# Two DiT blocks on one core: order of the first loads and of VectorE's first work

## The chip, the cores and the metric

The kernel runs on one core of one Trainium2 chip. The metric is the device time of one execution in microseconds (us). The engines of the core are TensorE (PE, matmuls, with its weight loads shown apart as PEld), VectorE (DVE), ScalarE (ACT), GpSimd (POOL) and SyncE (SP), which here only issues transfers (DMAs).

## The reference, cut to what matters

Two transformer blocks run one after the other on x of shape (1, 256, 1024), all in float32. Each has a feed-forward part, a mixing part and a second feed-forward part, and each part starts from a normalised x that is modulated by a scale and a shift computed from the vector c:

```
mods = (jax.nn.silu(c) @ w_ada[l] + b_ada[l]).reshape(B, N_MOD, D_MODEL)
n = modulate(rmsnorm(h, g_pre[l, 0]), shift(0), scale(0))      # x * (1 + scale) + shift
f = swiglu(n, w_ffn_gate[l, 0], w_ffn_up[l, 0], w_ffn_down[l, 0])
h = h + 0.5 * gate(0) * rmsnorm(f, g_post[l, 0])
```

The first matmul of the first feed-forward part therefore needs shift(0) and scale(0), that is silu(c) times the first 2048 columns of w_ada (1024 x 9216). The mixing part of the first block is an attention with a relative bias of 32 buckets, whose table is turned into Toeplitz rows at the start of the program; the rest of the program isn't touched by the change.

## The kernel before, in words

The 256 tokens are two tiles of 128 (T = 2), the model width 1024 is eight blocks of 128 (KD = 8). Weights are cut in pieces of 128 x 2048, loaded into w_raw (three slots) or e_raw, split into a rounded part (w_hi, by ScalarE) and a remainder (w_lo, by VectorE), and multiplied in three products on TensorE.

The program is written by hand, one instruction stream for each engine, with semaphores between them. The opening is the first 50 us or so:

- SP issues loads in the order in which they are written. All of SP's loads go through one queue (q1 in the profile), ScalarE's loads through another (q10).
- The first modulation is made in two halves of 512 columns of shift and of scale. Each half has eight "rows": row j holds w_ada's rows p*8 + j for all 128 partitions p, 128 x 1024 numbers, 512 KB (load_first, line 653). In the first half VectorE sums rows 0 to 6, each multiplied with a column of silu(c) (first_rows, lines 1525 to 1534), and TensorE sums row 7 (first_row, line 2173). In the second half VectorE has rows 0, 1, 4, 5, 6 and TensorE rows 2, 3, 7. The order lists are ON_DVE and ON_PE (lines 319 and 320).
- The sums over partitions are folded: VectorE reduces to 128 x 32 (line 1539, semaphore folded) and TensorE multiplies with the constant matrix pick (line 2171). VectorE then forms mod_col (lines 1549, 1557, 1559, semaphore first_mods), and normalised, transposed tokens go into nT (line 1276 on VectorE, line 881 on ScalarE).
- Tokens: both tiles of x are loaded into x_res (line 671, 512 KB each). ScalarE waits for both, squares them (line 865), GpSimd makes the reciprocal root, ScalarE scales them into y_row (line 1012). TensorE transposes y_row (line 1986).
- The small constants: ScalarE issues c_in, rel_in and onehot, makes silu(c) (c_act, semaphore c_ready), and issues ten more small loads (vec_rows, line 1002). VectorE spreads the relative bias table into rel_bc (line 1593, semaphore rel_ready) and builds pick from the identity that GpSimd made (lines 1596 and 1597, semaphore pick_ready). TensorE's first matmul (toe, line 2276) waits for rel_ready; then come 12 matmuls without use ("spins", line 2272), transposes of vec_rows (line 2281), 12 more spins, the first transposes of y_row, row 7, and the fold. ScalarE copies the toe product out (line 1006, toe_sb) ahead of its squares of the tokens.
- The opener weights are loaded behind the eight rows (load_opener, line 658), then a gate/up piece, then the second half's rows. Before row j of the second half SP waits until row j of the first half has been summed (first_sum, line 678; for row 7 fold_mm).

On VectorE the row that is summed first uses tensor_scalar (line 1531), the others scalar_tensor_tensor (line 1534). The lines of VectorE's opening are 1590 to 1602: before the change rows 0 and 1 come first, then the constants, then rows 2 to 6.

Of the kernel before, what the change touches and what calls it, by code (L numbers as in the profile page):

```python
# [17 lines left out]
KD = D // P  # L18
# [30 lines left out]
def program(nc, a, out):  # L49

    ctx = ExitStack()
    with ctx:
# [3 lines left out]
        def sem(name):  # L56
            return ctx.enter_context(nc.semaphore(name))
# [125 lines left out]
        c_ready = sem("c_ready")  # L183
# [135 lines left out]
        ON_DVE = [[0, 1, 2, 3, 4, 5, 6], [0, 1, 4, 5, 6]]  # L319
# [227 lines left out]
        def _(sp):  # L547
# [51 lines left out]
            def ffn_loads(f, next_e, next_b):  # L599
# [39 lines left out]
                for i, (_, b, _, post, _) in enumerate(gates[f]):  # L639
                    sp.dma_start(gate_in[:, 0, i, :], b.rearrange("(r q) -> r q", q=Q)).then_inc(gate_vecs, 16)  # L640
                    if post is not None:
                        sp.dma_start(gate_in[:, 1, i, :], post.rearrange("(r q) -> r q", q=Q)).then_inc(gate_vecs, 16)
# [10 lines left out]
            def load_first(half, j):  # L653
                dst = first_at[half][j].rearrange("p (m n) -> p m n", n=NB)
                cols = src[:, j, 0:2 * D].rearrange("p (m n) -> p m n", n=D)[:, :, half * NB:(half + 1) * NB]
                sp.dma_start(dst, cols).then_inc(first_loaded[j], 16)
# [8 lines left out]
                        cols = w.rearrange("(k p) n -> p k n", p=P)[:, 4 * half:4 * half + 4, 0:FC]  # L665
                        sp.dma_start(dst[:, k, g, :], cols[:, k]).then_inc(raw_loaded[s] if part else part_loaded, 16)

            for j in range(4):
                load_first(0, j)
            for t in range(T):  # L670
                sp.dma_start(x_res[:, t, :], a["x"][0, t * P:(t + 1) * P, :]).then_inc(x_loaded, 16)
            for j in range(4, KD):
                load_first(0, j)
            load_opener(0)
            load_gu("F0", 0, 1)
# [566 lines left out]
        def _(dve):  # L1242
# [47 lines left out]
            def fold_all(group):  # L1290

                f = group.split()[0]
                for half in range(len(ada_steps[f])):
                    dve.wait_ge(ada_done[half], n_ada[f] + KD)
                for i, (at, *_) in enumerate(fold_cols.get(group, [])):
                    last = fold(acc_flat, at, folds[:, i, :])
                for i in fold_gates.get(group, []):
                    last = fold(acc_flat, gates[f][i][0], gate_folds[:, i, :])
                last.then_inc(folded, 1)

            def mods_out(f):

                dve.wait_ge(fold_mm, FOLDS.index(f) + 1)
                for i, (_, blk, m, r) in enumerate(fold_cols.get(f, [])):
                    kind = 1 if m % 3 == 0 else 0
                    for a in range(P // Q):
                        rows = slice(a * Q, (a + 1) * Q)
                        last = dve.tensor_tensor(mod_col[rows, r, kind, :], ps[rows, fold_bank(f), i * Q + a:(i + 1) * Q:P // Q],
                                                 vec_col[rows, blk, KD * m:KD * m + KD], ALU.add)
                    link(last)  # L1310
                    if not kind:
                        g = gain_at.get(r, (0, 72))
                        link(dve.scalar_tensor_tensor(mod_col[:, r, 0, :], mod_col[:, r, 0, :], 1.0,
                                                      vec_col[:, g[0], g[1]:g[1] + KD], ALU.add, ALU.mult))

            def gate_out(group, i):
                f = group.split()[0]
                _, _, _, post, factor = gates[f][i]
                v = gate_row[:, i, :]
                dve.wait_ge(fold_mm, FOLDS.index(group) + 1)  # L1320
                dve.wait_ge(gate_vecs, 16 * n_vecs[f])
                link(dve.tensor_tensor(v, ps[0:Q, gate_bank(group), i * Q:(i + 1) * Q], gate_in[:, 0, i, :], ALU.add))
                if post is None:
                    dve.tensor_scalar(v, v, factor, None, ALU.mult).then_inc(gate_small, 1)
                else:
                    dve.scalar_tensor_tensor(v, v, factor, gate_in[:, 1, i, :], ALU.mult, ALU.mult).then_inc(gate_small, 1)
# [198 lines left out]
            def first_rows(half, js):  # L1525

                for j in js:
                    dve.wait_ge(first_loaded[j], 16 * (half + 1))
                    row, c = first_at[half][j], c_act[:, 0, j:j + 1]
                    if j == 0:  # L1530
                        dve.tensor_scalar(first_sums, row, c, None, ALU.mult).then_inc(first_sum, 1)
                        continue
                    dve.wait_ge(first_sum, len(ON_DVE[0]) * half + ON_DVE[half].index(j))
                    dve.scalar_tensor_tensor(first_sums, row, c, first_sums, ALU.mult, ALU.add).then_inc(first_sum, 1)
# [36 lines left out]
            def opening(half):  # L1571

                first_fold(half)
                if half == 0:
                    vectors()
                    dve.wait_ge(vec_ready, 2)
                first_folded(half)
                first_out(half)
                dve.wait_ge(first_mods, half + 1)
                pairs = (2 * half, 2 * half + 1)  # L1580
                for pair in pairs:
                    norm_cols("F0", 0, pair)
                for pair in pairs:
                    norm_lo("F0", 0, pair)
                opener_lo(half, 0)
                for pair in pairs:
                    norm_lo("F0", 1, pair)
                opener_lo(half, 1)

            dve.wait_ge(c_ready, 1)  # L1590
            first_rows(0, range(0, 2))
            dve.wait_ge(rel_loaded, 32)
            dve.tensor_copy(rel_bc[0:BUCKETS], rel_in[0:BUCKETS, :].rearrange("p (o h) -> p o h", o=1)
                            .broadcast_to([BUCKETS, P // H, H])).then_inc(rel_ready, 1)
# [1 line left out]
            link(dve.tensor_reduce(pick[:, 0:Q], ident[:].rearrange("p (r q) -> p q r", q=Q), AX.X, ALU.add))  # L1596
            dve.tensor_copy(pick[:, Q:P].rearrange("p (r q) -> p r q", q=Q),
                            pick[:, 0:Q].rearrange("p (o q) -> p o q", o=1).broadcast_to([P, P // Q - 1, Q])).then_inc(pick_ready, 1)
            first_rows(0, ON_DVE[0][2:])
            opening(0)  # L1600
            first_rows(1, ON_DVE[1])
            opening(1)
# [1110 lines left out]
```

## Time and profile before

| what | value |
|---|---|
| median of 3 runs | 1087.05 us (1086.76, 1087.05, 1090.59) |
| profiled execution | 1086.84 us |
| its span | 1085.1 us |
| PE busy | 1066.2 us, 98% |
| DVE busy | 854.0 us, 79% |
| ACT busy | 548.9 us, 51% |
| HBM read | 263.34 MB, 244 GB/s over the span |

The span goes from the first to the last instruction of the profile; the time of the execution also holds what lies around it. Busy shares are means over stages with different limits. In the rows below a start is in us from the start of the span, "x4" counts instructions, and the square brackets hold how long the engine had been idle and what ended it. Rows whose engine has a q (SPq, ACTq) are issues of transfers. The changed part is all in the first 20 us.

### The profile page before, as it was taken

To read this page: it belongs to the slowest core of one execution; us is meant where nothing else is said; L and a number is where in the kernel's file an instruction comes from. 1 tells how busy PE (TensorE), PEld (TensorE's weight loads), DVE (VectorE), ACT (ScalarE), POOL (GpSimd) and SP (SyncE) were. 2 spreads that over 40 slices of the span, in tenths; PEclk is the share of its full clock that TensorE was granted. 3 is DMA by queue.
4 is the path that set the end of the run, shared out by engine and by line. 5 is a ranking of instruction groups with operands and counts; after the bars stand their busy time and mean duration, and the time that the engine had idled before them with its cause. 6 is when DMAs were issued, how large, how long until landed. Compare 5 with 4: busy or idle time off the path is not lost.

```text
span 1085.1 us, 16394 instructions
## 1 busy us (share of the span) xinstructions
PE 1066.2 (98%) x6226; PEld 934.5 (86%) x6226; DVE 854.0 (79%) x939; ACT 548.9 (51%) x672; POOL 47.3 (4%) x78
## 2 busy tenths in 40 slices
PE   7999999999999999999999999999999999999997
PEld 6999999889988788888978888898887778888886
DVE  6889888778887888888878988876876787666665
ACT  5444343564765754444564444445654456444452
POOL 1000000011220100000010000000100000000001
PEclk9999999999999999999999999999999999999999
DMA  9999998556424599996569999844563536767651
GB/s 339 385 405 389 388 401 264 184 121 227 139 79 155 194 344 310 317 322 229 195 244 352 342 361 342 285 171 136 180 206 105 194 117 229 233 214 232 215 175 59
DMA packets 147205, 265.28 MB, mean 244 GB/s; under 512 B 9833, under 2 KB 104534, under 8 KB 142038
## 3 DMA queue, kind: packets, MB, share of 16 engines
q1 hardware_dynamic: 145440, 261.30, 70.0%
q0 software_dynamic: 1056, 3.17, 0.9%
q8 instruction: 31, 0.51, 0.2%
q10 hardware_dynamic: 662, 0.16, 0.1%
q14 instruction: 16, 0.13, 0.0%
HBM read 263.34 MB, written 1.27 MB: 244 GB/s over the span
## 4 chain that ended last, share of the span: by engine, by line
PE 89%; DVE 4%; ACT 3%; DMA 2%; issue 1%; POOL 1%; SPq 0%; POOLq 0%; DVEq 0%; ACTq 0%
PE ps L2035 18%; PE ps L1966 11%; PE ps L1967 11%; PE ps L1968 11%; PE ps L2041 10%; PE ps L2016 7%; PE ps L2018 6%; PE ps L2019 6%; DMA arena<-in_w_ada 2%; ACT w_hi L854 1%; PE ps L2567 1%; DVE y_row L1424 1%; DVE x_res L1430 1%; ACT y_row L870 1%; PE ps L2194 1%
## 5 line engine op out<-in xcount | busy, mean ns | idle before, releaser
L854 ACT ACTIVATE w_hi<-w_raw 128x2048 fp32r<-128x2048 f32 (+4 forms) x175 | 318.5, 1826 | 253.4 <-PE ps L1968 92.2
L1253 DVE TENSOR_TENSOR w_lo<-w_raw,w_hi 128x2048 fp32r<-128x2048 f32 (+1 forms) x160 | 360.2, 2253 | 101.5 <-ACT w_hi L854 100.7
L2035 PE MATMUL ps<-nT_both,w_hi 128*128 128x512 f32 x864 | 210.7, 391 | 0.0
L2035 PEld LDWEIGHTS ps<-nT_both,w_hi 128*128 128x128 f32 x864 | 158.8, 188 | 30.7
L2016 PE MATMUL ps<-nT_both,w_hi 128*128 128x256 f32 x576 | 165.3, 287 | 0.0
L2018 PE MATMUL ps<-nT_both,w_hi 128*128 128x256 f32 x576 | 163.7, 284 | 0.0
L2019 PE MATMUL ps<-nT_both,w_lo 128*128 128x256 f32 x576 | 163.7, 284 | 0.0
L1345 DVE SCALAR_TENSOR_TENSOR arena<-arena,c_act 128x3072 f32<-128x3072 f32 (+2 forms) x49 | 129.4, 2650 | 0.5 <-DMA arena<-in_ada_w 0.5
L1966 PE MATMUL ps<-w_hi,hT_hi 128*128 128x512 f32 x320 | 125.0, 391 | 0.0
L1967 PE MATMUL ps<-w_lo,hT_hi 128*128 128x512 f32 x320 | 125.0, 391 | 0.0
L1968 PE MATMUL ps<-w_hi,hT_lo 128*128 128x512 f32 x320 | 124.5, 389 | 0.0
L2041 PEld LDWEIGHTS ps<-nT_both,w_lo 128*128 128x128 f32 x864 | 114.3, 191 | 6.3
L2041 PE MATMUL ps<-nT_both,w_lo 128*128 128x256 f32 x864 | 116.3, 283 | 0.0
L2016 PEld LDWEIGHTS ps<-nT_both,w_hi 128*128 128x128 f32 x576 | 111.1, 193 | 0.8
L2018 PEld LDWEIGHTS ps<-nT_both,w_hi 128*128 128x128 f32 x576 | 111.2, 193 | 0.4
L2019 PEld LDWEIGHTS ps<-nT_both,w_lo 128*128 128x128 f32 x576 | 111.2, 193 | 0.0
L1966 PE MATMUL ps<-w_hi,nT_both 128*128 128x512 f32 (+2 forms) x228 | 88.5, 388 | 0.1
L1968 PE MATMUL ps<-w_hi,nT_both 128*128 128x512 f32 (+2 forms) x228 | 86.6, 380 | 0.0
L1967 PE MATMUL ps<-w_lo,nT_both 128*128 128x512 f32 (+2 forms) x228 | 86.5, 379 | 0.0
L1968 PEld LDWEIGHTS ps<-w_hi,hT_lo 128*128 128x128 f32 x320 | 60.1, 188 | 12.8
L1966 PEld LDWEIGHTS ps<-w_hi,hT_hi 128*128 128x128 f32 x320 | 60.2, 188 | 11.5
L1967 PEld LDWEIGHTS ps<-w_lo,hT_hi 128*128 128x128 f32 x320 | 60.2, 188 | 11.0
(327 smaller groups left out, 1264.1 us busy)
## 6 DMA issues: line engine op xcount, KB each, us to landing
arena<-in_w_ada SPq DMA_DIRECT2D x16, 1536.0 KB, 10.4
arena<-in_ada_w SPq DMA_DIRECT2D x16, 1536.0 KB, 8.6
w_raw<-in_w_in SPq DMA_DIRECT2D x44, 512.0 KB, 4.6
w_raw<-in_ffn_w_down SPq DMA_DIRECT2D x44, 512.0 KB, 4.2
w_raw<-in_w_ffn_down SPq DMA_DIRECT2D x42, 512.0 KB, 4.9
w_raw<-in_ffn_w_gate SPq DMA_DIRECT2D x42, 512.0 KB, 4.2
w_raw<-in_ffn_w_up SPq DMA_DIRECT2D x42, 512.0 KB, 5.2
w_raw<-in_w_ffn_gate SPq DMA_DIRECT2D x41, 512.0 KB, 7.2
```

What stands on the lines that cost most here:

```text
L854: copy = lambda o, i: act.activation(o, i, ACT.Copy)
L870: act.activation(y_row[:, t, cols], x_res[:, t, cols], ACT.Square, scale=D ** -0.5, accum_out=stat[:, 2 * n + t:2 * n + t + 1]).then_inc(s ...
L1253: dve.tensor_tensor(lo(s, n), raw(s, n), hi(s, n).bitcast(F32), ALU.subtract).then_inc(lo_ready[s], 1)
L1345: dve.scalar_tensor_tensor(acc, ada_raw[:, half, 0:n], c_act[:, blk, bass.ds(j, 1)], acc, ALU.mult, ALU.add)\
L1966: pe.matmul(o, xh, wh, start=start, stop=False, skip_group_check=True)
L1967: pe.matmul(o, xh, wl, start=False, stop=False, skip_group_check=True)
L1968: return pe.matmul(o, xl, wh, start=False, stop=stop, skip_group_check=True)
L2016: pe.matmul(o, hi(s)[:, cols], nT_hi[:, kk, :], start=(half == first_half and k == 0 and i % 2 == 0), stop=False, skip_group_check=True)
L2018: pe.matmul(o, hi(s)[:, cols], nT_lo[:, kk, :], start=False, stop=False, skip_group_check=True)
L2019: last = pe.matmul(o, lo(s)[:, cols], nT_hi[:, kk, :], start=False, stop=(half != first_half and k == 3), skip_group_check=True)
L2035: pe.matmul(ps[:, i, :], hi(s)[:, cols], nT_both[:, 4 * half + k].rearrange("p a n -> p (a n)"), start=(half == 0 and k == 0), stop=False, ...
L2041: last = pe.matmul(ps[:, i, 0:S], lo(s)[:, cols], nT_hi[:, kk, :], start=False, stop=(kk == KD - 1), skip_group_check=True)
```

## The change

SP: the two loads of the token tiles, which stood between rows 3 and 4 of the first half, now stand ahead of row 0. VectorE: the wait for silu(c) and rows 0 and 1 move behind the three constant instructions, so that the bias table and pick are made first and rows 0 to 6 then follow in one piece.

```diff
-            for j in range(4):
-                load_first(0, j)
             for t in range(T):
                 sp.dma_start(x_res[:, t, :], a["x"][0, t * P:(t + 1) * P, :]).then_inc(x_loaded, 16)
-            for j in range(4, KD):
+            for j in range(KD):
                 load_first(0, j)
             load_opener(0)
...
-            dve.wait_ge(c_ready, 1)
-            first_rows(0, range(0, 2))
             dve.wait_ge(rel_loaded, 32)
             dve.tensor_copy(rel_bc[0:BUCKETS], rel_in[0:BUCKETS, :].rearrange("p (o h) -> p o h", o=1)
                             .broadcast_to([BUCKETS, P // H, H])).then_inc(rel_ready, 1)
...
-            first_rows(0, ON_DVE[0][2:])
+            dve.wait_ge(c_ready, 1)
+            first_rows(0, ON_DVE[0])
             opening(0)
```

On SP, at the start of the program (x_res are the token tiles; arena and gate hold the eight rows of w_ada's first half; the difference, - before and + after; line numbers behind the edit are 2 lower):

```order
-L656 DMA arena<-in_w_ada 128x2x512 x4
-L671 DMA x_res<-in_x 128x1024 x2
-L656 DMA arena<-in_w_ada 128x2x512 x2
+L669 DMA x_res<-in_x 128x1024 x2
+L656 DMA arena<-in_w_ada 128x2x512 x6
 L656 DMA gate<-in_w_ada 128x2x512 x2
 L666 DMA arena<-in_w_ffn_gate 128x2x256
```

Two loads of 512 KB moved past four of 512 KB; what stands ahead of the fifth row is the same set as before, in another order.

On VectorE, at the start of the program, before the change (1531 and 1534 are the rows, 1593 is rel_bc, 1596 and 1597 are pick, 1539 is the fold):

```order
L1531 TENSOR_SCALAR arena<-arena,c_act 128x1024
L1534 SCALAR_TENSOR_TENSOR arena<-arena,c_act 128x1024
L1593 COPY arena<-arena 32x128
L1596 TENSOR_REDUCE arena<-ident 128x32
L1597 COPY arena<-arena 128x96
L1534 SCALAR_TENSOR_TENSOR arena<-arena,c_act 128x1024 x4
L1534 SCALAR_TENSOR_TENSOR arena<-gate,c_act,arena 128x1024
L1539 TENSOR_REDUCE arena<-arena 128x32
```

And after it:

```order
L1589 COPY arena<-arena 32x128
L1592 TENSOR_REDUCE arena<-ident 128x32
L1593 COPY arena<-arena 128x96
L1529 TENSOR_SCALAR arena<-arena,c_act 128x1024
L1532 SCALAR_TENSOR_TENSOR arena<-arena,c_act 128x1024 x5
L1532 SCALAR_TENSOR_TENSOR arena<-gate,c_act,arena 128x1024
L1537 TENSOR_REDUCE arena<-arena 128x32
```

The three constant instructions moved ahead of the first two rows; the rest keeps its order. On TensorE, ScalarE and GpSimd no instruction moved.

## Rows read from the trace of the kernel before

**Rows 1.** The page: engine, busy time, instructions; and the chain by engine.

```profile
PE 1066.2 (98%) x6226; PEld 934.5 (86%) x6226; DVE 854.0 (79%) x939; ACT 548.9 (51%) x672; POOL 47.3 (4%) x78
...
PE 89%; DVE 4%; ACT 3%; DMA 2%; issue 1%; POOL 1%; SPq 0%; POOLq 0%; DVEq 0%; ACTq 0%
```

**Rows 2.** Windows: length, busy by engine (instructions), granted clock, DMA share, GB/s.

```profile
0.00:50.00 50.00, 41.83 (x268) 38.02 (x269) 35.51 (x58) 23.23 (x37) 4.06 (x12) 0.97 1.02 359
38.00:42.00 4.00, 4.00 (x20) 3.92 (x20) 3.69 (x13) 3.17 (x7) 0.00 (x0) 0.57 1.08 385
```

**Rows 3.** The chain that ended last, first 60 us: start, length, what.

```profile
3.93 9.62 DMA arena<-in_w_ada
...
18.75 10.22 DMA arena<-in_w_ada
...
35.82 1.90 PE ps L2177 x18
```

**Rows 4.** Timeline of the issues by SP and ScalarE: start, length, queue, line.

```profile
0.81 1.98 SPq L656 DMA_DIRECT2D arena<-in_w_ada  x4
1.81 0.47 ACTq L991 DMA_DIRECT2D arena<-in_onehot  x1
2.83 1.06 SPq L671 DMA_DIRECT2D x_res<-in_x  x2
4.93 1.22 SPq L656 DMA_DIRECT2D gate<-in_w_ada  x2
15.45 3.25 SPq L656 DMA_DIRECT2D w_raw<-in_w_ada  x2
```

**Rows 5.** Issue to landing: row 0; one-hot table; the two tiles; rows 6, 7.

```profile
arena<-in_w_ada SPq DMA_DIRECT2D x1, 512.0 KB, 4.0
...
arena<-in_onehot ACTq DMA_DIRECT2D x1, 48.0 KB, 5.2
...
DMA to landing us min/median/max: 7.8/8.2/8.6
...
DMA to landing us min/median/max: 11.3/11.7/12.1
```

**Rows 6.** Timeline of PE, 7 to 30 us.

```profile
7.83 1.61 PE L2276 MATMUL ps<-arena 32*128 32x384 f32 x2 [7.83 <-DVE arena L1593]
9.37 5.21 PE L2272 MATMUL ps<-ones,ident 128*128 128x128 f32 x24
...
14.61 2.86 PE L2272 MATMUL ps<-ones,ident 128*128 128x128 f32 x24
17.30 0.60 PE L1986 MATMUL ps<-ident,y_row 128*128 128x128 f32 x4
17.74 1.84 PE L2177 MATMUL ps<-c_act,gate 128*128 128x1 f32 x16
...
29.01 0.60 PE L2177 MATMUL ps<-c_act,arena 128*128 128x1 f32 x4 [0.19 <-DMA arena<-in_w_ada]
```

**Rows 7.** Timeline of VectorE, 7 to 20 us.

```profile
7.47 0.21 DVE L1593 COPY arena<-arena 32x128 f32<-32x128 f32 x1
...
13.57 2.67 DVE L1534 SCALAR_TENSOR_TENSOR arena<-arena,c_act 128x1024 f32<-128x1024 f32 x2 [2.75 <-DMA arena<-in_w_ada]
...
19.94 0.69 DVE L1549 TENSOR_TENSOR mod_col<-ps,vec_col 32x8 f32<-32x8 f32 x4 [0.70 <-PE ps L2171]
```

**Rows 8.** Timeline of ScalarE, 12 to 20 us.

```profile
12.04 1.06 ACT L865 ACTIVATE y_row<-x_res 128x1024 f32<-128x1024 f32 x1 [2.07 <-DMA x_res<-in_x]
...
16.77 1.15 ACT L1012 ACTIVATE y_row<-x_res,stat 128x1024 f32<-128x1024 f32 x1 [1.37 <-POOL stat L780]
...
19.11 1.06 ACT L854 ACTIVATE e_hi<-arena 128x1024 fp32r<-128x1024 f32 x1 [1.18 <-DMA arena<-in_w_ffn_up]
```

**Rows 9.** ScalarE's queue, 3 to 5 us, then 9 to 12: packets, MB, share.

```profile
q10 hardware_dynamic: 166, 0.00, 4.7%
...
q10 hardware_dynamic: 217, 0.08, 10.4%
```

## The prediction

> **What bounds the kernel now.** I began with the busy times and the chain of the page [rows 1]: TensorE (PE) is busy 98% of the span and 89% of the chain runs through it, so a change of the opening is worth only what it takes from the time before PE's steady work. The table by stretch [rows 2] says how much that can be: in the first 50 us PE is busy 41.83 us. Of those 50 us, 8.2 are idle, and 7.83 of them lie ahead of PE's very first matmul [rows 6]. The DMA share is 1.02 over the same 50 us: the transfers never pause.
>
> Next the chain in order of time [rows 3]. Until 13.55 it is a transfer of the modulation rows, behind it VectorE works on two of them from 13.57 [rows 7], and from 18.75 it is again a transfer that lands at 18.75 + 10.22 = 28.97, which is when PE gets on (29.01, idle 0.19 [rows 6]). The last row of the second half is what PE works through from 35.82. So the opening is set by when w_ada's rows land, and these land in the order of SP's queue.
>
> The landing times follow from the issues [rows 4] and the flights [rows 5]. Row 0 of the first half lands at 0.81 + 4.0 = 4.8. The first token tile lands at 2.83 + 7.8 = 10.6, the second, issued just after 3.4, at 12.0. Row 4 lands at 13.55 (3.93 + 9.62 [rows 3]). Row 7, the one that PE sums itself, is the second of the two into gate: issued about 5.4, 12.1 in flight, 17.5. From row 0 to the second token tile there are 5 further transfers of 512 KB in 12.0 - 4.8 = 7.2 us, 1.44 us each; rows 5 to 7 take (17.5 - 13.55) / 3 = 1.32 us each.
>
> **The change part by part.**
>
> Two token tiles ahead of rows 0 to 3. No byte is added or taken away; six transfers of equal size change places. At 1.44 us each the tiles land at 4.8 and 6.2, rows 0 to 3 at 7.7, 9.1, 10.6 and 12.0. Row 4 has the same six transfers ahead of it and lands at 13.55 as before, and so does all behind it: row 7 at 17.5, the opener weights at 19.1, the second half's rows at 28.97 and after. Rows 0 to 3 come 2.9 us later. VectorE has 2.75 us idle ahead of row 4 [rows 7], which covers them: a row costs 2.67 / 2 = 1.34 us, less than the 1.44 between landings, so row 3 starts at about 12.0 and is done at 13.4, 0.15 us ahead of row 4. Cost 0. Should that cover fail, by row 3 landing 0.3 us later than I say, VectorE's sums end later one for one; but VectorE's fold is waited for only behind PE's own row (VectorE sits 0.70 us idle at 19.94 for PE's fold product), so up to 0.7 us even of that is free.
>
> SP. The second half's loads wait for first_sum and the buffers. Rows 0 to 3 done up to 2.9 us later makes the latest of them 13.4, while SP comes to the second half's rows only at 15.45 and to the first that reuses an arena buffer at 18.75 [rows 4]: 2.1 us and more to spare. In the first 10 us SP may fill its queue a little more slowly, but the queue is about 10 us deep (flights of 9.6 to 12.1 [rows 3, 5]), so no transfer starts late. Cost 0.
>
> ScalarE. Its squares waited 2.07 us for the tokens and started at 12.04; the second tile's scaling ended at 16.77 + 1.15 = 17.92 [rows 8]. Now the tokens are there at 6.2, but ahead of the squares on ScalarE stands the copy of the Toeplitz rows, which waits for PE's first matmul (7.83 + 1.61 = 9.44) and, with 384 columns, is below a square's 1.06 us. So the squares start between 9.4 and 10.5, and all of this ends some 2 us earlier. What is it worth? ScalarE then idles: it already had 1.18 us of idle at 19.11, waiting for the opener weights, whose landing doesn't move. And PE's transposes of tile 0 start at 17.30 because the spins end there, not because of y_row, whose tile 0 was scaled before 16.77. Gain 0.
>
> VectorE's copies ahead of row 0. The three constants (rel_bc, 0.21 us, and two small ones for pick, by estimate under 1 us together, since the largest reads an eighth of a row's numbers at 1.34 us a row) ran from 7.47 behind rows 0 and 1, with PE's first matmul waiting for the first of them [rows 6, 7]. Now they wait only for the small loads of ScalarE's queue. The one-hot table was issued at 1.81 and landed 5.2 later, 7.0 [rows 4, 5]. If this holds, the copy starts near 7.05, and PE and its chain of spins (5.21 + 2.86 us) move ahead by 0.4 us. That would free PE for row 7 at 17.3, but row 7 lands at 17.5 and needs 1.84 us of PE as before: PE gets on 0.1 to 0.2 us earlier, and at 28.97 it waits for the landing all the same. Gain at the end of the opening: 0. Row 0 lands at 7.7 and would start at 8.05 at the latest; at 1.34 us a row, rows 0 to 3 end at 13.4 in this case too.
>
> The other bound of the same edit: the copies now stand behind loads that share the engines with the token tiles. The landing of the one-hot table while 4 KB pieces flow isn't in this trace. From below: as before, 7.0. From above: if all of the time until the tiles are through (6.2 - 1.81 = 4.4 us) ran at half pace, 2.2 us later, 9.2; then PE's chain starts 1.8 us late, 0.19 of it is covered by the wait at 29.01, and the end moves by 1.6 us. Nearer rows are the packets of ScalarE's queue: 166 in the 2 us from 3 to 5, among rows of w_ada, and 217 in the 3 us from 9 to 12, while the token tiles flow [rows 9]: 83 against 72 per us, so a flight of 5.2 becomes 5.2 x 83 / 72 = 6.0 and the table lands at 7.8. I take the middle of 7.0 and 7.8, 7.4, which is where the copy starts today: shift of PE's chain 0, cost 0.
>
> The Trainium skill bears on this, in DMA: Bandwidth & Descriptors, section Queues, rings and completion order: each DMA engine takes turns between the queues that have work, one packet at a time. By that rule small loads wait behind longer packets, and the move would work against PE's first matmul. The trace agrees in direction, 72 against 83 per us, though the mix of packets differs between the two stretches. By the rule the sum would lie towards the late bound (+1.6 us), by the row at 0.
>
> Sum: 0 - 0 + 0 = 0.0 us on the span of 1085.1. Around the span lie 1086.84 - 1085.1 = 1.74 us. So the profiled execution would again be 1086.84; the median of the three runs is 0.2 above it, 1087.05. I say 1087.0.
>
> **The rivals.**
>
> A, the small loads come late (slower). The one-hot table and c land behind the token tiles, and the toe matmul, the 24 spins, PE's row 7 and the fold all move back. It decides as soon as the rel_bc copy starts later than 7.47 + 0.19 = 7.66. For it: the packet rate above, and that nothing else is ahead of the copy now. Against it: c's 4 KB and the table's 48 KB are little, and the tiles are through by 6.2. Full price +1.6, time 1088.4.
>
> B, PE's spins run at the slow pace for longer (slower). The same 24 records took 5.21 us first and 2.86 us behind that [rows 6]; the cause must lie in when PE's work begins. If a shift of the first matmul leaves one more such group at the slow pace, row 7 is reached 5.21 - 2.86 = 2.35 us later, less the 0.19 of cover: +2.2, time 1089.0. Against it: the shift is under half a microsecond.
>
> C, the stretch at low clock goes (faster). From 38 to 42 us the granted clock was 0.57 [rows 2], mostly the 1.2 GHz level, right behind PE's single-column sums from 35.82. At full clock that stretch would be 4 x (1 - 0.57) = 1.7 us shorter: 1085.1. For it: the pattern ahead of it could shift a little. Against: it is timed by landings that don't move.
>
> D, tokens were the limit after all (faster). If the earlier scaled rows let PE's transposes and folds begin 2 us earlier, 1085.0 would come out; against it stands row 7's landing at 17.5, 0.24 us ahead of PE's work on it at 17.74, and the wait at 29.01.
>
> **How the numbers follow.** Forecast (nothing moves, 1087.0) 0.66; A in some part 0.16; B 0.06; C 0.07; D 0.05. Beside these the shown runs themselves reach from 1086.76 to 1090.59, so a median of few runs can lie a microsecond or two off. The range goes from D's 1085.0 to B's 1089.0, with 0.1 above it. What a measurement can tell from no change is 0.5%, 5.4 us; no case here is worth half of that, so same 0.95, faster 0.02, slower 0.03 for what I have overlooked.
>
> **What would show it.** In the changed profile: token tiles landing by 6.3 and ScalarE's squares between 9.4 and 10.5, right behind the toe copy, not behind a transfer; row 3 landing near 12 and row 4 at 13.5 to 13.6 with VectorE's wait of 2.75 us spread over rows 0 to 3; PE's row 7 at 17.5 to 17.8; ScalarE's wait for the opener weights longer by what it gained, until 19.1 again; PE's wait ending at 29.0. The rel_bc copy within 7.0 to 7.8. I am wrong if row 4 or the second half's rows land more than 0.5 us from these times, or if PE reaches 29 us later than the landing there.

## The result, and the profile after

| | before | changed |
|---|---|---|
| median, 22 runs each | 1086.82 us | 1088.20 us |
| lowest to highest | 1086.52 to 1090.59 | 1086.44 to 1091.63 |
| profiled execution / its span | 1086.84 / 1085.1 | 1086.94 / 1085.2 |

The ratio changed to before is 1.0013, 95% interval 1.0007 to 1.0019: about 1.4 us slower. The profiled executions differ by 0.1 us only. So the loss isn't in this profile; it is in how often an execution is worse than it. Each timed run also gives its mean granted clock, and there the two kernels part. The table takes the changed kernel's 22 runs and 12 more of the third experiment, and 111 runs of before from the four batches of experiments. One run of before at 1318.96 us, with a mean clock of 0.751, is left out throughout.

| mean clock | before: runs, median (us) | changed: runs, median (us) |
|---|---|---|
| 0.996 and more | 91, 1086.85 | 15, 1086.93 |
| 0.994, 0.995 | 14, 1089.04 | 12, 1089.06 |
| 0.993 and less | 6, 1090.64 | 7, 1091.10 |

At equal clock both take about the same time. The share at 0.995 or less is 20 of 111 before and 19 of 34 now. With before's levels, these shares alone give a mean of 1086.85 + (14 x 2.19 + 6 x 3.79) / 111 = 1087.3 before and 1086.85 + (12 x 2.19 + 7 x 3.79) / 34 = 1088.4 for the changed kernel, whose 34 runs have a mean of 1088.5. The extra low-clock executions are the loss. "Low" means 0.995 or less from here on; where that limit decides a comparison, 0.996 is given too (3 of the 111 runs of before and 1 of the changed kernel's 34 are at 0.996).

The profile after, PE's timeline (start, length, engine, line; lines are 3 lower than before) answers to [rows 6]:

```profile
8.06 1.61 PE L2273 MATMUL ps<-arena 32*128 32x384 f32 x2 [8.06 <-DVE arena L1589]
9.60 4.93 PE L2269 MATMUL ps<-ones,ident 128*128 128x128 f32 x24
...
14.55 2.86 PE L2269 MATMUL ps<-ones,ident 128*128 128x128 f32 x24
17.25 0.60 PE L1983 MATMUL ps<-ident,y_row 128*128 128x128 f32 x4
17.89 1.95 PE L2174 MATMUL ps<-c_act,gate 128*128 128x1 f32 x16
...
29.84 0.50 PE L2174 MATMUL ps<-c_act,arena 128*128 128x1 f32 x4
```

and the weight load of row 7, which shows the wait that wasn't there before:

```profile
17.89 1.86 PEld L2174 LDWEIGHTS ps<-c_act,gate 128*128 128x128 f32 x16 [0.28 <-DMA gate<-in_w_ada]
```

PE now idles 0.28 us ahead of row 7. It was there as early as before (the transposes ahead of it start at 17.25 against 17.30); the row came later. The second half's first row, for which PE waited until 29.01 before, is reached only at 29.84 and without a wait. VectorE's and ScalarE's timelines answer to [rows 7, 8], first VectorE's, then ScalarE's:

```profile
7.70 0.21 DVE L1589 COPY arena<-arena 32x128 f32<-32x128 f32 x1 [7.70 <-DMA arena<-in_onehot]
...
12.46 4.10 DVE L1532 SCALAR_TENSOR_TENSOR arena<-arena,c_act 128x1024 f32<-128x1024 f32 x3 [0.31 <-DMA arena<-in_w_ada]
```

```profile
10.10 1.05 ACT L863 ACTIVATE y_row<-x_res 128x1024 f32<-128x1024 f32 x1
...
14.40 2.18 ACT L1010 ACTIVATE y_row<-x_res,stat 128x1024 f32<-128x1024 f32 x2
19.38 1.06 ACT L852 ACTIVATE e_hi<-arena 128x1024 fp32r<-128x1024 f32 x1 [2.81 <-DMA arena<-in_w_ffn_up]
```

The squares start at 10.10 behind the toe copy, both tiles are scaled by 16.6 instead of 17.9, and ScalarE then waits 2.81 instead of 1.18 us for the opener weights: the earlier tokens bring nothing. The rel_bc copy now starts when the one-hot table lands. The windows (length, busy by engine, then granted clock, DMA share, GB/s) answer to [rows 2]:

```profile
19.00:24.00 5.00, 5.00 (x33) 5.00 (x32) 4.07 (x16) 3.79 (x7) 0.00 (x0) 0.66 1.09 356
38.00:42.00 4.00, 3.69 (x28) 3.23 (x28) 2.95 (x12) 2.26 (x6) 0.00 (x0) 1.00 1.07 384
```

The stretch at the 1.2 GHz level lies between 20 and 24 us here, behind row 7, and not at 38 to 42. Each profile has one such stretch of 3 to 4 us, which is why their spans agree.

### The profile page after: what moved, and what is told of

It is laid out like the page before. It is cut to its first block, busy times and chain, and to the rows that moved or that the text cites. A ratio compares the mean times of both kernels' runs of the same rounds, so it can differ in the third digit from the quotient of the medians.

```text
span 1085.2 us, 16394 instructions
## 1 busy us (share of the span) xinstructions
PE 1066.0 (98%) x6226; PEld 934.3 (86%) x6226; DVE 853.9 (79%) x939; ACT 548.8 (51%) x672; POOL 47.1 (4%) x78
## 4 chain that ended last, share of the span: by engine, by line
PE 90%; DVE 4%; ACT 3%; issue 1%; POOL 1%; DMA 1%; ACTq 0%; POOLq 0%; DVEq 0%
PE ps L2032 18%; PE ps L1963 11%; PE ps L1964 11%; PE ps L1965 11%; PE ps L2038 10%; PE ps L2013 7%; PE ps L2016 6%; PE ps L2015 6%; PE ps L2191 1%; PE ps L2269 1%; ACT w_hi L852 1%; PE ps L2564 1%; DVE y_row L1422 1%; DVE x_res L1428 1%; PE ps L2174 1%
```

## The experiments

Each was timed in 11 or 12 runs beside the kernel before, except two single executions (11 and 12). "Low" is the number of runs at a mean clock of 0.995 or less, the next column the number at 0.996. Experiments 1 to 4, 5 to 8, 9 to 12 and 13 to 14 ran on four different chips, where before had 8 of 35, 8 of 35, 2 of 21 and 2 of 20 low; the changed kernel's 12 runs of experiment 3 are on the first of them.

| kernel | median | mean | low | at 0.996 | idle of PE's weight loads ahead of row 7 in its profile |
|---|---|---|---|---|---|
| before (111 runs) | 1086.8 to 1086.9 by batch | 1087.3 | 20 of 111 | 3 | 0 |
| changed (34 runs) | 1088.2; 1088.7 | 1088.5 | 19 of 34 | 1 | 0.28; 1.09 |
| 1 tokens first alone | 1089.28 | 1089.26 | 0 of 12 | 0 | 0 |
| 2 constants first alone | 1086.95 | 1087.89 | 3 of 12 | 0 | 0 |
| 4 transposes early | 1087.19 | 1087.44 | 0 of 12 | 3 | 0 |
| 5 before, 8 spins | 1086.88 | 1087.71 | 4 of 12 | 0 | 0.66 |
| 6 changed, 16 spins | 1087.72 | 1087.82 | 1 of 12 | 3 | 0 |
| 7 changed, spins between sums | 1087.53 | 1088.22 | 3 of 12 | 0 | 0 |
| 8 changed, transposes between sums | 1087.47 | 1087.85 | 2 of 12 | 0 | 1.33 |
| 9 before, 4 spins | 1087.53 | 1088.41 | 5 of 11 | 0 | 1.54 |
| 10 row 0 as gate | 1087.39 | 1087.39 | 0 of 11 | 1 | 0 |
| 13 before, 14 spins | 1086.96 | 1086.93 | 0 of 11 | 0 | 0.51 |
| 14 row 0 as gate, 10 spins | 1086.92 | 1087.46 | 2 of 11 | 0 | 0.32 |

**1, 2: each part alone.** The edits are the first and the second hunk of the change.

> SP's part of the change alone: both token tiles ahead of row 0, VectorE as before. Clock theory: what costs time is not a constant delay but a stretch of half granted clock (3.6 us) that in some executions falls into PE's thin stretch around row 7 (17.9 to 20 us) and onto the products behind it, because the rows of w_ada land about 0.3 us later and PE idles ahead of row 7. Then this kernel shows the spread of the changed one: median 1 to 2 us above before, single runs 1088 to 1091. Delay theory: only a fixed 0.1 to 0.3 us, with single runs as close together as those of before (1086.5 to 1087.1). If the trouble comes from VectorE's part (the later first matmul), this kernel times like before.

> VectorE's part alone: constants ahead of row 0, loads in the order of before. The rel_bc copy should start when the one-hot table lands, about 7.0 to 7.7, first matmul within 0.3 us of 7.83; row 0, there at 4.9, now waits behind the copies, VectorE still has its 2.75 us of idle ahead of row 4. Clock theory: row 7 lands at 17.5 as before, PE has no idle ahead of it, so times like before (1086.8, tight). Rival (the later start of PE's first matmul is to blame): spread as in the changed kernel.

With the tokens first and VectorE as before, the kernel is slower, ratio 1.0016 (1.0006 to 1.0025), but in another way than either theory said: no low-clock run at all, and a delay of all its runs (lowest 1087.79). In its profile (span 1087.1) VectorE comes to the bias table late:

```profile
10.64 0.21 DVE L1591 COPY arena<-arena 32x128 f32<-32x128 f32 x1
```

Rows 0 and 1 land about 3 us later and the constants stand behind them; the copy is at 10.64 instead of 7.47, PE's stream starts at 10.99 and reaches row 7 at 20.22. So the second hunk is needed to make up for the first. The second alone times as before: 1.0003 (0.999 to 1.0016), though its copy starts at 6.97 in the profile, earlier than in any with rows 0 and 1 first. So the second hunk by itself isn't shown to raise the share of low-clock runs (3 of 12 beside 8 of 35).

**3: the changed kernel again.**

> The changed kernel itself beside the others on one chip, for the spread of its runs and for a second profile. Clock theory: runs from 1086.5 to 1091, and if this profile is of a slower run, its half-clock stretch lies elsewhere than 20.3 to 24 us or there are two of them. Delay theory: all within 0.3 us of 1087.0.

The median is 1088.70, with 7 of 12 low and runs from 1085.95 to 1091.38; the ratio to before is 1.0011 (1.0 to 1.0023). The profile, of one of the short executions (1086.93), has the half-clock stretch from 19.6 to 23 and the idle ahead of row 7 is four times as long:

```profile
17.82 1.86 PEld L2174 LDWEIGHTS ps<-c_act,gate 128*128 128x128 f32 x16 [1.09 <-DMA gate<-in_w_ada]
```

**4, 6, 7, 8: the gap filled, or the sums thickened.**

```diff
 # 4: eight transposes ahead of row 7 (after y_row, before first_row)
             norm_transposes("F0", 0, range(2))
+            norm_transposes("F0", 1, range(2))
+            norm_transposes("F0", 0, range(2, PAIRS))
...
             first_fold(0)
-            norm_transposes("F0", 1, range(2))
-            norm_transposes("F0", 0, range(2, PAIRS))
...
 # 6: more spins ahead of the first transposes
-            spin(12)
+            spin(16)
...
 # 7: between row 7's sums (8: the transposes of 4 in the place of spin)
-                for _ in first_row(0, j):
-                    pass
+                for i, _ in enumerate(first_row(0, j)):
+                    if i % 2 == 0:
+                        spin(1)
```

> The changed kernel with eight more token transposes (tile 1 pairs 0 and 1, tile 0 pairs 2 and 3) ahead of row 7 on TensorE instead of behind the fold; both scaled tiles are ready by 16.6. They take about 0.9 us and fill the 0.28 us of idle, so row 7 starts 0.4 to 0.6 us later than 17.89, but thin work is shorter on its far side too: fold and then only four transposes and the spins. Clock theory: it can go either way on the placing of the half-clock stretch; if idle ahead of row 7 is what matters, the spread shrinks towards before (median 1086.8 to 1087.3). Delay theory: row 7 later by 0.5, so 0 to 0.4 us slower than the changed kernel, same tight spread.

> The changed kernel with 16 instead of 12 spins in the same place: PE has no idle ahead of row 7, and starts it up to 0.7 us later than 17.89. Clock theory: the share of low-clock runs falls from 19 of 34 to that of before (a quarter) and the median to 1086.9 to 1087.3. Landing theory: 0.3 to 0.7 us slower than the changed kernel, spread unchanged.

> The changed kernel with one spin behind every second of row 7's eight single-column sums (4 spins, about 0.95 us more of PE ahead of the fold). The wait ahead of row 7 stays. Clock theory in its strong form (what matters is the thin stretch as a whole): no half-clock stretch at 20 to 24 in the profile, low-clock runs at or below a quarter, and the floor of the times 0 to 0.6 us higher because the fold is later. If idle alone matters, the spread stays that of the changed kernel. Landing theory: 0.5 to 1.0 us slower than the changed kernel.

> The changed kernel with the eight transposes of the fourth experiment put between row 7's sums, two behind every second sum, so that row 7 starts when it lands and thin work alternates with full matmuls. Adds no work. Clock theory: like the seventh experiment in clock, fold near 20.5 against 19.9, median 1086.9 to 1087.3 with few low-clock runs. Landing theory: as the changed kernel or 0.3 us slower.

Filling the gap (4, 6) brings the share of low-clock runs down: 0 and 1 of 12 against 19 of 34 with the same loads, and on the same chip 0 of 12 (4) against 7 of 12 (3). The limit of 0.995 flatters this, since three more runs of each, at 1088.21 to 1089.19 us, are at 0.996. Counted up to 0.996, experiments 4, 6 and 10 together have 8 of 35, the changed kernel 20 of 34 and before 23 of 111: about the share of before, and not none. Filling costs a little too, since the fold is later; with 16 spins the copy happened to start at 7.96 in the profile and row 7 at 18.92. The landing theory asked for times of up to 0.7 us above the changed kernel's; both medians (1087.19, 1087.72) are below its 1088.2. In 7 and 8 the sums are thickened, and they have 3 and 2 of 12, which settles nothing: the profile of 7 has no idle ahead of row 7, that of 8 has 1.33 us. All four intervals against before include 1. The profiles of 4 and 6 are both of executions at 0.996 (1088.79 and 1089.19 us, spans 1087.1 and 1087.5), and each has one stretch of about twice the usual length, with a mean of 0.57 over the window from 37 to 45 us, first 4, then 6:

```profile
37.00:45.00 8.00, 8.00 (x37) 7.53 (x37) 5.81 (x16) 5.93 (x12) 0.00 (x0) 0.57 1.08 377
...
37.00:45.00 8.00, 8.00 (x39) 7.61 (x39) 5.72 (x16) 5.68 (x11) 0.00 (x0) 0.57 1.08 377
```

**5, 9: the gap made in the kernel before.** The same line with 8, then 4 spins; loads and VectorE untouched.

> The kernel before with 8 instead of 12 spins (matmuls without use) ahead of the first transposes. Loads and VectorE stay as they were; PE only reaches row 7 about 0.9 us sooner than 17.64 and idles until it lands at 17.5. Clock theory (idle ahead of row 7, then single-column sums, brings a stretch of half granted clock behind it, in part of the executions): the share of runs with a mean clock of 0.995 or less rises from 8 of 35 to about half, the median to 1087.5 to 1089. Landing theory (the 0.3 us later landings of w_ada's rows cost the time): nothing moves, 1086.9 and 8 of 35.

> The kernel before with 4 instead of 12 spins ahead of the first transposes: PE should idle 1.3 to 1.8 us ahead of row 7 (the 8-spin kernel had 0.42 in its profile and 4 of 12 runs at a mean clock of 0.995 or less, not clearly more than the 16 of 70 of the kernel before). Idle theory: with this much idle the share of low-clock runs is above half and half-clock stretches appear at 19 to 25 us, as in both profiles of the changed kernel. If the share stays at a quarter, idle ahead of row 7 is not enough to explain the changed kernel.

With 8 spins nothing clear: 4 of 12, ratio 1.0003 (0.9993 to 1.0013), and I had expected half. With 4 spins the changed kernel's behaviour appears: 5 of 11 low (before 2 of 21 on that chip), ratio 1.0013 (1.0003 to 1.0023). The edit takes eight full matmuls out as it makes the idle, so it can't tell the one from the other. This profile is of a low-clock execution, span 1088.9, clock 0.992. From its timeline, the weight loads of row 7:

```profile
17.69 2.21 PEld L2177 LDWEIGHTS ps<-c_act,gate 128*128 128x128 f32 x16 [1.54 <-DMA gate<-in_w_ada]
```

and two of its windows (granted clock is the third number from the end):

```profile
19.00:26.00 7.00, 7.00 (x33) 6.81 (x33) 5.60 (x17) 5.38 (x11) 0.00 (x0) 0.51 1.08 366
39.00:47.00 8.00, 8.00 (x37) 7.44 (x37) 6.14 (x17) 4.74 (x11) 0.00 (x0) 0.57 1.09 392
```

There are two long stretches. The first begins while PE works on row 7's single-column sums, right behind the idle, the second at the end of the sums of the second half. Both cost time, as PE's second fold and the first products with w_lo behind it show, here and then in the kernel before:

```profile
39.91 0.61 PE L2171 MATMUL ps<-arena 128*128 128x32 f32 x2
47.15 0.62 PE L2194 MATMUL ps<-w_lo,nT_both 128*128 128x512 f32 x2
...
37.59 0.39 PE L2171 MATMUL ps<-arena 128*128 128x32 f32 x2
43.39 0.62 PE L2194 MATMUL ps<-w_lo,nT_both 128*128 128x512 f32 x2
```

PE is 2.3 us behind at the fold and 3.8 us behind at the products, the same 3.8 us by which the span is longer (1088.9 against 1085.1).

**10, 14: the start tied to row 0.** Changed loads, but row 0 summed ahead of the constants; 14 with 10 spins instead of 12.

```diff
+            dve.wait_ge(c_ready, 1)
+            first_rows(0, range(0, 1))
             dve.wait_ge(rel_loaded, 32)
...
-            dve.wait_ge(c_ready, 1)
-            first_rows(0, ON_DVE[0])
+            first_rows(0, ON_DVE[0][1:])
```

> The changed kernel with row 0 summed ahead of the constants, as a gate in front of them: the rel_bc copy then starts behind row 0 (lands about 7.7), near 8.4, whatever the one-hot table does, the first matmul near 8.75, row 7 without idle near 18.5. Jitter theory (the copies start when the one-hot table happens to land, 6.6 to 8.0 in the profiles so far, and this moves PE's whole stream against row 7's landing): the runs come together, few at low clock, and all about 0.5 us above 1086.9. If not, about half of the runs stay at low clock as in the changed kernel.

> The changed loads with row 0 as a gate in front of the constants and 10 instead of 12 spins: row 7 starts near 18.4 instead of 18.89, without idle. Idle theory: as few low-clock runs as in the tenth experiment (0 or 1 of 12, against 19 of 34 of the changed kernel, though loads and their order are the same), and 0.2 to 0.5 us faster than it: median 1086.9 to 1087.2. Loads theory (the order of the loads itself brings the low clock, or a fixed delay): a third or more of the runs at low clock, or no time below 1087.2.

10 has 0 of 11 low and 1087.39, as the idle theory said (row 7 at 18.89, no idle), though its runs still reach from 1085.92 to 1088.39. 14 has the expected median, 1086.92, but 2 of 11 low, one more than I had allowed. In its profile the first 24 spin records took 4.28 us, PE was ready before row 7 landed after all (idle 0.32 ahead of 17.42, where I had expected none ahead of 18.4), and the stretch lies at 20 to 24 again.

**11, 12: two more profiles of the changed kernel.**

> The changed kernel unchanged, one more look. About half of its executions are at a mean clock of 0.995 or less. If this one is, clock theory says its profile has a second stretch of half clock, or one of twice the length, within 19 to 50 us, and the span is longer by what it costs there; if it is a fast one, one stretch at 19 to 24 or at 38 to 42.

> The changed kernel unchanged, a further look, for the same question: where the half-clock stretches of a slower execution lie, and when the one-hot table landed in it (idle of VectorE ahead of the rel_bc copy).

Both were at a high clock (1086.82 and 1087.41), so a low-clock execution of the changed kernel itself was never seen in a profile. What they show is how far PE's arrival at row 7 wanders. The eleventh:

```profile
8.87 4.22 PE L2269 MATMUL ps<-ones,ident 128*128 128x128 f32 x24
...
17.93 1.86 PEld L2174 LDWEIGHTS ps<-c_act,gate 128*128 128x128 f32 x16 [1.72 <-DMA gate<-in_w_ada]
```

and the twelfth:

```profile
18.27 1.86 PEld L2174 LDWEIGHTS ps<-c_act,gate 128*128 128x128 f32 x16 [0.83 <-DMA gate<-in_w_ada]
```

The first spins take 4.2 us in one execution and 5.2 in the other, and the one-hot table landed at 6.96 and 7.22, after 7.70 and 6.90 in the two earlier profiles. Row 7 starts at 17.82 to 18.27, each time when it lands. Together the idle of the weight loads is 0.28, 1.09, 1.72 and 0.83 us in four profiles, never zero. The longest of them, 1.72 us in the eleventh, has no half-clock stretch behind it; that execution has its stretch at 38 to 43. So the idle doesn't bring the early stretch each time.

**13: margin for the kernel before.** 14 spins instead of 12.

> The kernel before with 14 instead of 12 spins ahead of the first transposes: row 7 starts near 18.1 instead of 17.64, well behind its landing at 17.5. Idle theory: the kernel before stands on the edge (0.14 us between landing and start) and its own low-clock runs (18 of 91 with a mean clock of 0.995 or less) come from executions in which row 7 lands later than PE is ready; with this margin there are 0 or 1 of 12, mean at or below 1087.2, median 1086.9 to 1087.3 (the fold is up to 0.5 us later, 0.19 of it covered). If 2 or 3 of 12 are at low clock still, that share has another cause.

0 of 11 low, median 1086.96, highest 1087.35, where the 20 runs of before beside it had 2 at low clock; the ratio is 1.0 (0.999 to 1.0009). The count came out as the idle theory said, the profile didn't. In its profile (span 1084.6) the spins took the short time, 4.27 us, and even with 14 of them the weight loads waited 0.51 us; there was no stretch of half clock before 60 us, here in the window of the first 50:

```profile
0.00:50.00 50.00, 41.30 (x277) 36.59 (x278) 36.13 (x58) 23.23 (x38) 4.06 (x12) 1.00 1.02 359
```

PE's stream reached the second half's products at 40.53 and waited there for ScalarE:

```profile
40.53 2.21 PE L2194 MATMUL ps<-w_hi,nT_both 128*128 128x512 f32 x8 [0.31 <-ACT nT_both L854]
```

Of the versions tried this is the one to keep: no faster in the median, and without the runs at 1089 to 1091 in what was measured. That it is free of them isn't shown. At the share of before, 20 of 111, eleven runs without one come up about one time in nine, and the profile has idle ahead of row 7 and so not the margin that was meant. Experiments 1, 4, 6 and 10 start row 7 later and have no idle there in their profiles; with them it is 1 of 58 up to 0.995, but 8 of 58 up to 0.996, against 23 of 111.

## Why the prediction was wrong

The mechanics were right for the most part. Rows 0 to 3 came late and VectorE's idle of 2.75 us took most of it: row 3 was started at 12.46 and not at 12.0, and the sums ended 0.3 us later (the fold's first step at 17.98 against 17.67), which was covered, as the prediction said it would be, by PE's own row. The constants' copy started at 6.90 to 7.70 in four profiles, about the forecast span of 7.0 to 7.8 (6.59 to 7.96 with the variants that have the same loads and the constants first); the squares came at 10.10 and ScalarE gave all of it back. Tokens weren't the limit (rival D). SP was a little late: it came to the second half's rows at 15.73 instead of 15.45. Rival A was decided by its own sign in the profile, a copy later than 7.66 (it started at 7.70), without its price, since the first spins took 4.93 instead of 5.21 us; its far bound of 9.2 was never near.

The step that failed is the one on the copies: "PE gets on 0.1 to 0.2 us earlier, and at 28.97 it waits for the landing all the same. Gain at the end of the opening: 0." I booked PE's idle ahead of row 7 as free, since row 7's landing sets the time, and put the clock at no change. What the runs show in its place is a larger share of low-clock executions, 19 of 34 against 20 of 111, worth 1.4 us, and in the profile PE at the second half's first row at 29.84, behind the landing, which the prediction had named as a sign of being wrong. What changed ahead of it is the idle in front of row 7, with 1.9 us of single-column sums behind it. Of the 16 profiles, 9 have idle ahead of row 7, and 5 of these have a stretch at the 1.2 GHz level that begins between 19 and 21 us; of the 7 without idle none has one there. Experiment 9 makes this idle with the loads of before and gets the same ratio, 1.0013; experiments 4, 6 and 10 take it away with the changed loads and come back to about the share of before.

That the idle is the cause is likely, but not shown. Experiment 9 also has fewer full matmuls ahead of row 7, and 4, 6 and 10 also start row 7 later, at 18.35 to 18.92. Experiments 5, 8, 11 and 13 have 0.66, 1.33, 1.72 and 0.51 us of idle and no early stretch in their profiles. And 11 of the 16 profiles have a stretch behind the second half's sums, to which PE comes without idle. No kernel kept the idle while it moved only the time of row 7 or the matmuls ahead of it.

I kept row 7's landing at 17.5, and that is where the idle comes from in part. Worked out from issue and flight, it landed at 17.5 to 17.8 in the five profiles with the old order of loads and at 17.3 to 18.6, on average 17.9, in the eleven with the new one. So it comes some 0.3 us later and wanders by more than the 0.24 us of margin (17.74 against 17.5). The copy wanders as well: with the loads of before and rows 0 and 1 ahead of it it started at 7.42 to 7.74 (four profiles), with the constants first it follows the one-hot table. Each hunk adds its part, and neither alone gave the changed kernel's share of low-clock runs.

Rival B had about the right size (+2.2 us, and the low groups are at +2.2 and +3.8) and the wrong cause: I tied it to spins at a slow pace for longer, with a chance of 6%, and the first 24 records took 4.2 to 5.5 us in all profiles. Its time is also counted from 1086.84; from the forecast of 1087.0 it is 1089.2, above the top of the range that it was to set. Rival C priced the stretch at 38 to 42 at 1.7 us. Experiment 13 had an execution without it, and its span is 0.5 us shorter than before's: at full clock PE only reaches the wait for ScalarE sooner. Even these 0.5 us are less than executions of before at a high clock differ among themselves (1086.23 to 1087.60). One short stretch costs about as much at either place (span 1085.1 with it at 38, 1085.2 with it at 20); what costs are long ones (1087.1 and 1087.5 with one, 1088.9 with two).

And I took one profile and three times for the kernel. The single time at 1090.59 was in front of me; I named it beside the range, which has 0.1 us above rival B, but gave it no mechanism. The forecast of no change within 0.5% holds, and the median of 1088.2 lies inside my range; that of 0.0 us doesn't hold. The range was built from rivals that didn't come about, so that it holds the median is luck.

Left open: a profile of the changed kernel in a low-clock execution, why 7 and 8 are in between, and whether it is the idle, the later start of row 7 or the work ahead of it that counts.

## What to carry to other kernels

Where an engine waits for data that sets the time anyway, look at what it does just before and after: in this kernel an idle gap of TensorE next to thin matmuls (one column) went with a loss larger than the gap, later, and in some executions only. A margin read from one profile can be smaller than what the landing and the start differ by from one execution to the next; here it was 0.24 us against about 1 us. Where the times of a kernel form groups, compare the shares of the groups and their mean clocks before comparing two profiles, and see whether the result survives a shift of the limit between the groups.

## What the runs showed of the hardware

- With the loads and the order of before or of the changed kernel, the median times go with the mean granted clock: at 0.996 to 0.998 1086.9 us, at 0.994 to 0.995 1089, at 0.993 and less 1090.6 to 1091.1.
- A half-clock stretch within the first 50 us was there in 15 of the 16 profiles; it began between 19.1 and 20.8 us (5 profiles) or between 37.5 and 39.8 us (11, one of them with both), each time within the last microsecond of about 2 us of single-column sums or within 1.4 us behind them. Ahead of the sums at 38 PE had no idle. A stretch lasted 3 to 4 us, in three of the profiles (4, 6 and 9) about twice that.
- The same first 24 spin records took 4.2 to 5.5 us in different executions, though the granted clock of the profile reads 1.00 there; where 24 more came behind them, these took 2.86 to 3.01.
